# Streaming one weight matrix through a six-slot ring: chunks of two k tiles by 512 columns, used four at a time, in place of chunks of one k tile by 1024 columns, used two at a time

## What is computed

```
mod = silu(cvec) @ w_ada + b_ada          # (2, 1024) @ (1024, 6144), w_ada differs per layer
sh1, sc1, g1, sh2, sc2, g2 = split(mod, 6)
h = rms_norm(x, norm1_g) * (1 + sc1) + sh1
x = x + g1 * mixer(h)                     # pooling, 2-D neighbourhood attention, convolution, differential attention
h = rms_norm(x, norm2_g) * (1 + sc2) + sh2
x = x + g2 * peer_ffn(h)                  # product-key experts, 128 gathered rows per token
```

## Time and profile before

| | us |
|---|---|
| median of 3 runs | 5075.87 (5073.49 to 5084.46) |
| time of the profiled execution | 5075.87 |
| its span, first to last instruction | 5074.1 |
| tensor engine (PE) busy | 4401.1 (87%) |
| vector engine (DVE) busy | 3388.2 (67%) |
| mean granted TensorE clock | 0.971 of full speed |

### The profile page before, as it was taken

How to read it: one execution, slowest core, us unless ns; L and a number is a source line. 1 busy time by engine, 2 the same in 40 slices (tenths; PEclk the granted TensorE clock), 3 DMA queues, 4 the chain that set the end, 5 groups by cost and what they waited for, 6 DMA issues and landing times.

```text
span 5074.1 us, 46885 instructions
## 1 busy us (share of the span) xinstructions
PE 4401.1 (87%) x14388; PEld 2272.8 (45%) x14388; DVE 3388.2 (67%) x7266; ACT 1950.9 (38%) x5074; POOL 1662.3 (33%) x1600
## 2 busy tenths in 40 slices
PE   7999899998899888888888998999789987777877
PEld 4774465446555433344544445643464522222222
DVE  4259766777786676774444996777778767576544
ACT  1211644442343434665533035544323433333333
POOL 3004212232343453443333322233224444443432
PEclk9999999998999999999999998999999999999999
DMA  8852537998899999999998242399979999999998
GB/s 289 297 164 96 185 129 288 352 355 319 341 420 420 417 420 420 406 398 417 399 420 355 74 151 98 111 357 342 345 305 420 409 422 422 421 421 420 418 421 356
DMA packets 277115, 1677.27 MB, mean 331 GB/s; under 512 B 31808, under 2 KB 31856, under 8 KB 112384
## 3 DMA queue, kind: packets, MB, share of 16 engines
q0 software_dynamic: 190896, 1365.43, 66.7%
q1 hardware_dynamic: 82944, 302.03, 16.3%
q10 hardware_dynamic: 3024, 6.82, 0.3%
HBM read 1667.33 MB, written 6.82 MB: 330 GB/s over the span
## 4 chain that ended last, share of the span: by engine, by line
DMA 36%; PE 33%; DVE 17%; ACT 7%; issue 5%; POOL 0%; DVEq 0%; SPq 0%; ACTq 0%; POOLq 0%
DMA arena<-experts,bsb 26%; PE ps L2245 13%; DMA arena<-experts,peidx 10%; PE ps L1824 5%; DVE arena L1516 4%; DVE arena L1728 3%; PE ps L1932 2%; PE ps L2011 2%; DVE arena L1417 2%; PE ps L2097 2%; PE ps L2119 2%; ACT L1076 1%; ACT T L1080 1%; PE ps L2136 1%; DMA wring<-w 1%
## 5 line engine op out<-in xcount | busy, mean ns | idle before, releaser
L2245 PE MATMUL ps<-arena,T 128*128 128x512 f32 x4096 | 1966.3, 614 | 445.7 <-ACT T L1080 444.7
L1728 DVE CUSTOM_DVE_ANT_0 arena<-arena,h_sb 128x1024 f32<-128x1024 f32 x1024 | 1253.0, 1227 | 858.1 <-DMA arena<-experts,bsb 854.9
L684 POOL DMA_INDIRECT arena<-experts,bsb x1024 | 1095.6, 1070 | 1742.5 <-PE ps L2245 1587.4
L2245 PEld LDWEIGHTS ps<-arena,T 128*128 128x128 f32 x4096 | 724.8, 191 | 1570.2 <-ACT T L1080 951.8
L1076 ACT ACTIVATE bsb<-T 128x1 f32<-128x1 f32 x1024 | 205.8, 201 | 1309.4 <-DVE T L1728 1307.8
L1824 PE MATMUL ps<-h_sb,wring 128*128 128x256 f32 (+2 forms) x2304 | 515.6, 381 | 29.4 <-DVE h_sb L1481 12.0
L2156 PE MATMUL ps<-h_sb,wring 128*128 128x512 f32 x1024 | 460.7, 604 | 34.2 <-DVE arena L1653 32.0
L667 POOL DMA_INDIRECT arena<-experts,peidx x224 | 249.7, 1115 | 655.6 <-DVE arena L1417 584.2
L1824 PEld LDWEIGHTS ps<-h_sb,wring 128*128 128x128 f32 x2304 | 379.8, 196 | 176.8 <-issue 145.9
L1080 ACT ACTIVATE T<-ident,bsb 128x128 f32<-128x128 f32 x1024 | 410.9, 401 | 33.5
L1407 DVE CUSTOM_DVE_ANT_0 arena<-arena,h_sb 128x1024 f32<-128x1024 f32 x256 | 312.8, 1223 | 117.2 <-DMA arena<-experts,peidx 116.3
(11 more groups left out here) (326 smaller groups left out, 4519.9 us busy)
## 6 DMA issues: line engine op xcount, KB each, us to landing
wring<-w SPq DMA_DIRECT2D x576, 512.0 KB
arena<-experts,bsb POOLq DMA_INDIRECT x1024, 15.3
bsb<-bias POOLq DMA_DIRECT2D x16, 512.0 KB, 4.0
arena<-subk POOLq DMA_DIRECT2D x4, 1024.0 KB, 8.4
arena<-experts,peidx POOLq DMA_INDIRECT x256, 7.9
arena<-v_scratch POOLq DMA_DIRECT2D x64, 64.0 KB, 2.1
x_sb<-xT POOLq DMA_DIRECT2D x1, 2048.0 KB, 14.0
v_scratch<-arena ACTq DMA_DIRECT2D x8, 256.0 KB, 2.0
```

What stands on the lines that cost most here:

```text
L684: gp.indirect_dma_start(rows[:, n % NS, :], None, experts, bass.IndirectOffsetOnAxis(ap=eidx[:, t % 2, i:i + 1], axis=0)).then_inc(row_in[ ...
L1728: v.tensor_tensor_reduce(e, e, htok(t), 1.0, 0.0, ALU.mult, ALU.add, dots[:, t % 2, i:i + 1]).then_inc(dot, 1)
L2245: mm = pe.matmul(ps[:, 6 + half, :], diag[:, n % ND, :], rows[:, n % NS, D + half * 512:D + (half + 1) * 512], start=(i == 0), stop=(i == ...
```

## The change

A chunk of "A" becomes two k tiles for one g: chunk 16n + 4q + g holds k tiles 2q and 2q + 1 of block g. The number, the size and the order of the transfers stay as they are; the host packs `w_ada` in the other order. A part is now one of four per group, and works through four chunks. With width 4 it waits for all four chunks and then issues eight matmuls (g = 0..3 with k tile 2q, g = 0..3 with k tile 2q + 1), and all four chunks are released by the last four. With width 2 (group 0 of layer 0 alone) it takes two chunks at a time. The prompt has 8 parts behind steps 40, 43, 46, 49, 52, 55, 58, 61 in place of 16, the latent attention 12 behind jobs 17, 19, ... 39 in place of 24. The `modulation_columns` keep their places.

```diff
-            def modulation_part(l, n, k):
-
-                if k == 0:
+            def modulation_part(l, n, q, width):
+
+                if q == 0:
                     need(pe, ada_rows, ADA_GROUPS * l + n - 1)
-                c0 = 16 * n + 2 * k
-                for c in (c0, c0 + 1):
-                    wait_chunk(pe, "A", l, c)
-                for g in range(4):
-                    c = c0 + g // 2
-                    mm = pe.matmul(ps[32 * g:32 * g + 32, row_bank(l, n), :], csil32[:, k, :], chunk_of("A", l, c)[:, g % 2 * 512:(g % 2 + 1) * 512],
-                                   start=(k == 0), stop=(k == KD - 1), skip_group_check=True)
-                    if g % 2:
-                        mm.then_inc(used("A", l, c), 1)
-                if k == KD - 1:
-                    for c in (c0, c0 + 1):
-                        wait_used(pe, "A", l, c)
+                for g0 in range(0, 4, width):
+                    chunks = [16 * n + 4 * q + g for g in range(g0, g0 + width)]
+                    for c in chunks:
+                        wait_chunk(pe, "A", l, c)
+                    for kk in range(2):
+                        for g, c in enumerate(chunks, g0):
+                            mm = pe.matmul(ps[32 * g:32 * g + 32, row_bank(l, n), :], csil32[:, 2 * q + kk, :], chunk_of("A", l, c)[:, kk * 512:(kk + 1) * 512],
+                                           start=(q + kk == 0), stop=(q + kk == 4), skip_group_check=True)
+                            if kk:
+                                mm.then_inc(used("A", l, c), 1)
+                if q == 3:
+                    for g in range(4):
+                        wait_used(pe, "A", l, 16 * n + 12 + g)
                     pe.sem_inc(ada_row, 1)
...
-            for k in range(KD):
-                modulation_part(0, 0, k)
+            for q in range(4):
+                modulation_part(0, 0, q, 2)
...
-            ada_at = {K_ADA + 3 * part // 2: part for part in range(2 * KD)}
             for k in range(K_RMS1 + 2, PSTEPS):
                 next(mixer)
-                if k in ada_at:
-                    modulation_part(0, 1 + ada_at[k] // KD, ada_at[k] % KD)
+                part = (k - K_ADA) // 3
+                if (k - K_ADA) % 3 == 0 and 0 <= part < 8:
+                    modulation_part(0, 1 + part // 4, part % 4, 4)
...
-                    if l + 1 < DEPTH and n > NDIFF:
-                        part = n - NDIFF - 1
-                        if part < KD * ADA_GROUPS:
-                            modulation_part(l + 1, part // KD, part % KD)
-                        if part and part % KD == 0 and part // KD <= ADA_GROUPS:
-                            modulation_columns(l + 1, part // KD - 1)
+                    if l + 1 < DEPTH and n > NDIFF and (n - NDIFF) % 2:
+                        part = (n - NDIFF) // 2
+                        if part < 4 * ADA_GROUPS:
+                            modulation_part(l + 1, part // 4, part % 4, 4)
+                        if part and part % 4 == 0 and part // 4 <= ADA_GROUPS:
+                            modulation_columns(l + 1, part // 4 - 1)
```

More of the change, by code:

```diff
@@ L2287 @@
     order = (0, 2, 1, 3)
-    stream, small, rowg, lamrow = [a["w_ada"][l].reshape(KD, P, 3, 2, 1024).transpose(2, 0, 3, 1, 4).reshape(NADA, P, 1024) for l in range(DEPTH)], [], [], []
+    stream, small, rowg, lamrow = [_row_chunks(a["w_ada"][l]).reshape(3, 4, 4, P, 1024).swapaxes(1, 2).reshape(NADA, P, 1024) for l in range(DEPTH)], [], [], []
     for l in range(DEPTH):
```

## The result

The changed kernel takes 5122.31 us (median of 4 runs, 5119.49 to 5133.56), the kernel before 5074.68 beside it: ratio 1.0086, 95% interval 1.0066 to 1.0105. It is 47.6 us slower. The forecast was 5095.4, with a range of 5079 to 5107: the direction was right, the size (19.5 us) less than half of what was measured. All 16 executions of the changed kernel recorded here lie between 5108.72 and 5141.26, with a median of 5119.2. The profiled execution is one of the longer ones (5126.3) and has a span of 5124.5, against 5074.1.

The account below looks back on a forecast made before the run. The prediction took the chunk ring, with almost no slack, as the bound in two of three stages. Start 0.9, prompt 11 and latent stage 7.6 summed to 19.5 us on 5075.87, giving 5095.4 us, range 5079 to 5107.

Parts of the forecast that it names:

- Slots come back late, two in flight; the ring sets the pace: Prompt and latent stages: four chunks released at a part's end, two in flight meanwhile, so the next part waits for refill.
- 5.5 us from part end to part start: Ring refill in prompt and latent stages: issue, second chunk's landing and PE's start take 5.5 us, bounds 4.5 and 8.0.
- The latent parts at the full clock: Latent stage: every part counted at 1.9 us, period 7.4 where two jobs took 6.37; +7.6 us.
- A part costs PE 1.9, 3.7 at the low clock: Each new part on PE: 1.9 us at full clock, about 3.7 at the lower clock.
- Prompt stage, +11: Prompt of layer 0: parts start 5.5 us after the previous one ends, moving the branch projections later by 11 us.
- PE's saving of 3.6: Latent stage, PE work alone: 24 x 1.15 = 27.6 us becomes 12 x 2.0 = 24.0, 3.6 us less.
- Start +0.9: Start: the last pair of chunks takes 1.9 us where it took 1.0, directly ahead of the prompt's norm; +0.9 us.
- Shifts pass whole: Behind the prompt and latent stages: nothing absorbs the delays, so they reach the end of the program in full.
- Short landings: Rival: a refill's two chunks land 4.5 us behind the release; total 5081 us; chance 0.24.
- PE's saving: Rival: chunks land within 4.1 us, PE never waits in the latent stage; total 5070 us; chance 0.06.
- Colder and later: Rival: prompt parts 2 to 5 at 1.2 GHz, bias collisions in the latent stage (period 8.0); 5106 us; chance 0.15.
- The rule that the Trainium skill gives: Ring refill: about 2.0 us fixed plus bytes at 436 GB/s, so the second chunk lands 4.4 us behind the release.

Follow-up runs that it names:

- old_joint: Kernel before with its old chunk packing, but outside the start each part waits for four chunks and releases all four together; 5117.62 us, ratio 1.0072.
- old_pairs: Kernel before with its parts standing in twos at the changed kernel's places, each with its own waits and releases; 5088.29 us, ratio 1.002.
- fill: Changed kernel with eight matmuls on constants ahead of each four-chunk part, so PE works where it waited; 5116.7 us, ratio 1.0061.
- r7_after: Changed kernel with a ring of seven slots, room made by dropping tables (output not the reference's); 5098.15 us, ratio 1.003.
- after_again: The changed kernel measured once more, nothing altered; 5120.79 us, ratio 1.0075.
- latent_joint: Kernel before with four-chunk waits and releases, old packing, in the latent attention alone; prompt as before; 5099.35 us, ratio 1.0035.
- no_bias: Changed kernel without the bias loads of heads 2 to 7 of layer 0, old bias data added instead; 5107.28 us, ratio 1.005.
- start_w4: Changed kernel with width 4 in the first group too; 5108.16 us in one run.

## Why the prediction was right in direction and wrong in size

- *Slots come back late, two in flight; the ring sets the pace.* Right, and shown: old_joint has the cost without the new packing, old_pairs takes away most of the cost by waiting for the slots and giving them back in pairs, and the cost follows the number of slots (65, 40, 24 us).
- *5.5 us from part end to part start.* The term was mis-sized in the latent stage, as one number for two cases. Measured are 5.0 to 5.1 when nothing else is under way and 6.2 to 7.2 with a bias, 5.96 on average. I had written collisions into a rival and left them out of the sum. That is 11 times 0.46 = 5.1 us of the 11.5 by which the latent stage (19.1) exceeds the forecast (7.6). In the prompt the term was right in sum: six refills took 32.8, counted were 33.0.
- *The latent parts at the full clock.* The larger share of the latent stage's miss, and not in the sum at all. Two parts that began at the lower clock (759.14 and 792.51) took 3.4 and 3.3 in place of 1.9: 2.9 us. The last part and the job behind it at the lower clock took 7.8 (824.67 to 832.47), where 4.0 were counted: 3.8. With 5.1 that is 11.8, less some 0.4 for parts of 1.85 in place of 1.9.
- *A part costs PE 1.9, 3.7 at the low clock.* Right (1.85; 3.64); what failed is how many of them I counted at the lower clock: two, where nine ran wholly or mostly there.
- *Prompt stage, +11.* Measured 18.7. The series of starts held for five parts (122.3, 129.7, 137.1, 146.3, 155.5 forecast; 122.3, 130.1, 138.2, 146.4, 156.6 measured), then I let the clock go up. It stayed low on average (0.67 and 0.71 in the windows): parts 4, 5 and 6 took 3.6, 3.3 and 3.6 where I counted 1.9. So part 6 came at 173.65, not 170.3: 3.4 us, and 1.7 more for its own length. 2.4 us more were steps between that part and the sums of step 59 (177.3 to 179.75) that I set to nothing, although the trace of before has 2.1 there too (157.2 to 159.26). 3.4 + 1.7 + 2.4 = 7.5, which is what 194.73 lies above the 187.2 of the series. From the sums to the branch projections it took the 15.0 that I had worked out (179.75 to 194.73). fill shows that the clock is part of it: with PE kept at work the projections start 5.9 earlier.
- *The clock behind the latent stage.* The step that was not in the sum at all. In the first profile it cost 15.1 us and in r7_after's as much, in after_again, old_joint and latent_joint nothing to speak of. Whether it comes differs from run to run, so it is no fixed part of the 47.6; without it the miss is still there (39.7 in after_again, against 19.5).
- *PE's saving of 3.6.* Real as work, but swallowed by waits: with the ring late, of PE's work only the part itself is on the path, since the refill starts at its end.
- *Start +0.9.* Measured 0.8.
- *Shifts pass whole.* Right: 0.6 us between the stages and -3.8 behind them, in a tail that varies by 17 anyway.
- *The rivals.* Short landings and PE's saving were wrong: the earliest refill took 4.9, not 4.5 or 4.1. For a refill beside which nothing else is under way, though, the 4.5 were as near as my own 5.3; it was the biases that decided. "Colder and later" was the right mechanism, with a period of 8.0 near the measured 8.1; I gave it 0.15, and its total of 5106 lacked the clock behind the latent stage, and took 4 too few in the prompt (15 for 18.7) and 5 in the latent stage (14 for 19.1).
- *The rule that the Trainium skill gives* (DMA: Bandwidth & Descriptors, Anatomy of one DMA) made it 4.4 from release to the second landing, as an estimate from its figures; the section gives them for transfers that GpSimd issues, the ring's are issued from SP. The trace shows 4.9 at best: near when nothing else is under way, and short by 2.5 when another transfer is (6.9); the measurement decides.

Still open is what is left between the stages' sum and the medians: in after_again the latents' branch projections start 36.0 later than in the first profile of before, the medians on that chip differ by 39.7. Since the tail varies by more than that, and the two are from different chips, I can't place these 3.7 us.

## What to carry to other kernels

Count a ring like this one not by its slots but by what is in flight while a consumer works: slots less what one step holds until its end. When a step takes more of the ring at a time, the refill's latency, about 5 to 7 us here for two chunks, comes onto the path once per step, even if the bytes, the work and the mean rate are the same. And when a wait appears ahead of TensorE, price the work behind it at the lower clock in the sum, not in a rival.

## What the runs showed of the hardware that I had not expected

A busy PE does not show that the clock comes up. From 830 to 840 us of the first profile PE is busy 10.0 of 10 us at a granted clock of 0.50 (1.2 GHz), and it stays there to 868, with the same jobs that run at 1.00 in after_again with PE busy 10.0 of 10. r7_after has the same from 808 to 850. What differed is the clock at which the stretch was entered. In these two the last part came behind 2.39 and 3.38 us of waiting and ran wholly at the lower level (3.64 us); in after_again it came behind 2.13 and ran at the full one (1.92). The length of the wait alone does not decide it: in no_bias and start_w4 the last part came behind 2.79 and 3.05 us and began low too, but took 3.56 and 3.61, so that the clock came up about at its end, and the jobs behind it ran at 1.00. A wait of 2 to 3 us may thus cost 15 us or nothing. What decides between the two, these five profiles don't show.

What the earlier trace rows had shown also holds for twice the work: matmuls on four blocks of columns go side by side. Eight take 1.85 us, where one alone takes 0.86.
